# First attention of block 1: heads in pairs, one softplus function, the values' product behind queries and keys, head norms in small steps

## The reference, cut to what matters

```python
h = rms_norm(x, mix_norm_g[l]);  proj = h @ w_in[l]
sb_q, sb_k, sb_v, sw_q, sw_k, sw_v, gate_logits = jnp.split(proj, split_at, axis=-1)
o_sb = stick_breaking_attention(...)      # 8 heads of 64; per head, s < t only:
    z = q k^T * scale
    log_keep = where(strict, -softplus(z), 0)
    tail = reverse cumsum over keys of log_keep, less log_keep
    w = where(strict, exp(log_sigmoid(z) + tail), 0);  o = w v
q = apply_rope(rms_norm(sw_q heads)); k = apply_rope(rms_norm(sw_k heads))
y_swa = sliding_window_sink_attention(q, k, sw_v, sinks[l]) @ w_branch_swa[l]
gates = sigmoid(gate_logits)              # 2 x 1024 columns
x = x + (gates[0] * (o_sb @ w_branch_sb[l]) + gates[1] * y_swa) @ w_out[l]
```

## Time and profile before

| | |
|---|---|
| median of 3 runs | 2334.74 us (2334.29 to 2335.71) |
| profiled execution, its own time | 2335.98 us |
| its span in the profile | 2334.3 us |
| granted TensorE clock, mean | 0.997 of full speed |
| PE / PEld / DVE / ACT / POOL busy | 98 / 86 / 64 / 50 / 8 % |
| mean HBM traffic | 170 GB/s |

### The profile page before, as it was taken

One profiled execution on the slowest core, in us unless ns is written; L12 is line 12 of the kernel. 1 busy time (PEld: TensorE's weight loads), 2 busy tenths in 40 slices (PEclk: granted clock), 3 DMA queues, 4 the chain that ended last, 5 costly groups with the idle time before them and its releaser, 6 DMA issues.

```text
span 2334.3 us, 35415 instructions
## 1 busy us (share of the span) xinstructions
PE 2280.2 (98%) x14356; PEld 2015.2 (86%) x14370; DVE 1489.5 (64%) x2026; ACT 1157.4 (50%) x1785; POOL 198.3 (8%) x191
## 2 busy tenths in 40 slices
PE   7999999999999999999999999999999999999998
PEld 6898888888888888799999878888888999987887
DVE  4557855646874775665667677668655665776774
ACT  4845444574543544545443554445444445355543
POOL 0001200001110210000004001011100000220110
PEclk9999999999999999999999999999999999999999
DMA  7335565533666665554534555566655444364654
GB/s 227 110 115 175 186 201 179 156 112 123 192 189 197 215 191 191 175 177 153 164 100 151 184 165 188 189 208 199 190 175 184 161 158 126 104 215 148 186 185 140
DMA packets 108995, 395.73 MB, mean 170 GB/s; under 512 B 12375, under 2 KB 12545, under 8 KB 108577
## 3 DMA queue, kind: packets, MB, share of 16 engines
q1 hardware_dynamic: 104400, 377.53, 50.7%
q0 software_dynamic: 4432, 15.93, 2.1%
HBM read 392.92 MB, written 1.05 MB: 169 GB/s over the span
## 4 chain that ended last, share of the span: by engine, by line
PE 92%; ACT 4%; DVE 2%; issue 1%; DMA 1%; SPq 0%; DVEq 0%; ACTq 0%
PE psum L409 55%; PE psum L538 17%; PE psum L537 9%; PE psum L837 3%; PE psum L871 2%; PE psum L762 2%; PE psum L855 1%; DMA ring<-in_weights 1%; ACT w_high L363 1%; DVE w_low L366 1%; PE psum L1879 1%; ACT L1338 0%; DVE xT L721 0%; ACT xT L715 0%; DVE x L630 0%
## 5 line engine op out<-in xcount | busy, mean ns | idle before, releaser
L366 DVE TENSOR_TENSOR w_low<-ring,w_high 128x1024 fp32r<-128x1024 f32 x704 | 863.6, 1237 | 512.3 <-ACT w_high L363 510.5
L363 ACT ACTIVATE w_high<-ring 128x1024 fp32r<-128x1024 f32 x704 | 734.5, 1055 | 484.9 <-DMA ring<-in_weights 483.6
L538 PE MATMUL psum<-xT,w_high 128*128 128x512 f32 x1728 | 607.5, 396 | 0.0
L537 PE MATMUL psum<-xT,w_low 128*128 128x256 f32 x1728 | 485.4, 281 | 0.0
L409 PE MATMUL psum<-xT,w_high 128*128 128x256 f32 x2496 | 462.4, 287 | 0.0
L409 PEld LDWEIGHTS psum<-xT,w_high 128*128 128x128 f32 x2496 | 391.6, 193 | 0.8
L538 PEld LDWEIGHTS psum<-xT,w_high 128*128 128x128 f32 x1728 | 324.2, 188 | 77.6
L409 PE MATMUL psum<-w_high,hidden 128*128 128x512 f32 x1216 | 376.7, 390 | 0.0
L409 PE MATMUL psum<-xT,w_low 128*128 128x256 f32 x1248 | 354.4, 284 | 0.0
L537 PEld LDWEIGHTS psum<-xT,w_low 128*128 128x128 f32 x1728 | 326.5, 189 | 0.2
L409 PEld LDWEIGHTS psum<-w_high,hidden 128*128 128x128 f32 x1216 | 228.2, 188 | 47.2
(11 more groups left out here) (237 smaller groups left out, 2309.7 us busy)
## 6 DMA issues: line engine op xcount, KB each, us to landing
ring<-in_weights SPq DMA_DIRECT2D x706, 512.0 KB, 3.6
pages<-in_affine POOLq DMA_DIRECT2D x16, 512.0 KB, 5.8
ring<-in_weights SPq DMA_DIRECT2D x8, 440.0 KB, 3.2
pages<-in_gains POOLq DMA_DIRECT2D x4, 512.0 KB, 4.8
pages<-in_mem POOLq DMA_DIRECT2D x2, 1024.0 KB, 5.6
ring<-in_weights SPq DMA_DIRECT2D x4, 384.0 KB, 3.1
x<-in_x_in SPq DMA_DIRECT2D x2, 512.0 KB, 4.8
pages<-in_rows POOLq DMA_DIRECT2D x2, 512.0 KB, 5.8
```

The costliest lines, as they stand in the source:

```text
L363: eng.activation(high, raw, ACT.Copy).then_inc(self.flag("w_rounded").sem, 1)
L366: eng.tensor_tensor(self.w_low[:, piece % SLOTS, 0:width], raw, high.bitcast(F32), ALU.subtract).then_inc(self.flag("w_split").sem, 1)
L537: pe.matmul(out[:, 0:SEQ], low, self.xT_high[:, k, :], start=(k == 0), stop=False, skip_group_check=True)
L538: m = pe.matmul(out, high, self.xT[:, k, :, :].rearrange("p x s -> p (x s)"), start=False, stop=(k == kn - 1), skip_group_check=True)
```

## The change

The three activations of softplus become one, `ACT.Softplus`, and DVE takes the larger of it and max(z, 0) in place of the sum. Heads go in pairs on all engines: two heads' logits, the values of the two before, a gate, the two heads' sums, a gate. Nine gates stand in the first attention (0 to 8) in place of eleven; gates 10 and 11 go beside the window attention, into steps 1 and 3, and gate 12 into step 5. The product `sbv` goes behind `sbq` and `sbk`, with its pieces in the stream, its banks and its copies on ACT (these now after the roots). `window_heads` yields more often (after the variances, and after the norm of each token tile), and its steps start earlier, from the queries on.

```diff
-GATES_SB = [[0, 1], [2], [3], [4], [5], [6], [7], [8], [9]]
-BESIDE_SWA = {0: [("ysb", 1)], 1: [("gate", 12)], 2: [("ysb", 2)], 4: [("ysb", 3)], 6: [("gate", 13)]}
+BESIDE_SWA = {0: [("ysb", 1)], 1: [("gate", 10)], 2: [("ysb", 2)], 3: [("gate", 11)], 4: [("ysb", 3)],
+              5: [("gate", 12)], 6: [("gate", 13)]}
...
# stream_1, the banks and PE: "sbv" moves from before "sbq" to behind "sbk"; gates in the new order
...
@@ PE
-            for h in range(10):
-                if h < 8:
-                    logits(h)
-                if 1 <= h <= 8:
-                    later_keys(h - 1)
-                if h < 9:
-                    for n in GATES_SB[h]:
-                        gate(n)
-                if h >= 2:
-                    sb_values(h - 2)
-            gate(10)
+            for h in range(0, 8, 2):
+                for x in (h, h + 1):
+                    logits(x)
+                if h:
+                    for x in (h - 2, h - 1):
+                        sb_values(x)
+                gate(h)
+                for x in (h, h + 1):
+                    later_keys(x)
+                gate(h + 1)
+            for x in (6, 7):
+                sb_values(x)
+            gate(8)
...
@@ ACT
             c.root(act, l, c.rsum[:, :, :])
             c.root(act, l, c.fac[:, :, 0:2])
+            split(c.piece_after["sbv"] + AHEAD - 1)
+            for t in range(NT):
+                act.activation(sbv[:, t, :], c.filled(act, l, banks, ("sbv", t)), ACT.Copy ...
...
-                act.activation(b, c.psum[:, 4 + h % 2, 0:SEQ + P], ACT.Abs)...
-                act.activation(b, b, ACT.Exp, scale=-1.0)...
-                act.activation(b, b, ACT.Ln, bias=1.0).then_inc(*c.flag("sb_ln").one())
+                act.activation(soft[:, h % 2, 0:SEQ + P], c.psum[:, 4 + h % 2, 0:SEQ + P], ACT.Softplus
+                               ).then_inc(*c.flag("sb_soft").one())
...
+            for h in range(0, 8, 2):
+                for x in (h, h + 1):
+                    softplus(x)
+                if h:
+                    gate(h - 1)
+                else:
+                    after("sbv")
+                for x in (h, h + 1):
+                    weigh(x)
+                gate(h)
+            gate(7)
+            gate(8)
...
@@ DVE
+            for n in range(2):
+                dve.tensor_scalar(sbqT ... ("sbq", n) ...
+                after(("sbq", n))
+                next(side)
+            for n in range(2):
+                after(("sbk", n))
+                next(side)
             next(side)
...
+            split(c.piece_after["sbv"] + AHEAD - 1)
+            for h in range(0, 8, 2):
+                for x in (h, h + 1):
+                    dve.wait_ge(*c.flag("sb_soft").at(l, x + 1))
+                    if h:
+                        dve.wait_ge(*c.flag("sb_summed").at(l, x - 1))
+                    dve.scalar_tensor_tensor(kept[:, x % 2, ...], psum, 0.0, soft, ALU.max, ALU.max)...
+                after(("gate", h - 1) if h else "sbv")
                 next(side, None)
+                after(("gate", h))
+                next(side, None)
```

More of the change, by code:

```diff
@@ L113, in branch @@
                 s.add(("ysb", n, k), "w_branch_sb", k * P, span(n * P, P), split=True)
-    gates(0, 12)
+    gates(0, 10)
     branch(0, 4)
-    gates(12, 13)
-    branch(4, 8)
-    gates(13, 16)
+    gates(10, 11)
+    branch(4, 6)
+    gates(11, 12)
+    branch(6, 8)
+    gates(12, 16)
     s.matrix("ysw", "w_branch_swa", 512, span(0, D), P, split=True)
@@ L1073, in block_1 @@
     banks, BOTH = Banks(), ("act", "dve")
-    for key in ("swq", "swkv", "sbv"):
+    for key in ("swq", "swkv"):
         for t in range(NT):
             banks.add((key, t))
-    for key, first, end in (("sbq", 0, 2), ("sbk", 0, 2), ("gate", 0, 12), ("ysb", 0, 2), ("gate", 12, 13), ("ysb", 2, 4),
-                            ("gate", 13, 16), ("ysw", 0, 4)):
+    for key, first, end in (("sbq", 0, 2), ("sbk", 0, 2), ("sbv", 0, 2), ("gate", 0, 10), ("ysb", 0, 2), ("gate", 10, 11), ("ysb", 2, 3),
+                            ("gate", 11, 12), ("ysb", 3, 4), ("gate", 12, 16), ("ysw", 0, 4)):
         for n in range(first, end):
@@ L1228, in _ @@
                      swq[:, t, (2 * i + j) * P:(2 * i + j + 1) * P]) for j in range(2) for t in range(NT)])
-            gate(11)
+            gate(9)
             c.wait_read_out(pe, l, "osb0", "osb1")
@@ L1305, in _ @@
             after("swkv")
[L1306 to L1310, removed]
             after(("sbq", 0))
@@ L1321, in _ @@
             c.root(act, l, c.fac[:, :, 0:2])
+            split(c.piece_after["sbv"] + AHEAD - 1)
+            for t in range(NT):
+                act.activation(sbv[:, t, :], c.filled(act, l, banks, ("sbv", t)), ACT.Copy
+                               ).then_inc(*c.drained(banks, ("sbv", t)))
             def softplus(h):
@@ L1426, in after @@
                 split(c.piece_after[key] + AHEAD)
[L1428 to L1439, removed]
             def window_heads():
@@ L1474, in window_heads @@
                         yield
+            c.norm_vector(dve, l, 0, c.x, c.xs,
+                          first_rows if l == 0 else lambda t, n: add("down", l - 1, t, n), gain, None, split, -1,
+                          lambda: dve.wait_ge(*c.flag("gain_in").at(l, 16)))
             side = window_heads()
+            for key in ("swq", "swkv"):
+                after(key)
             next(side)
-            next(side)
[L1480 to L1490, removed]
+            for n in range(2):
+                dve.tensor_scalar(sbqT[:, 2 * n:2 * n + 2, :].rearrange("p k s -> p (k s)"),
+                                  c.filled(dve, l, banks, ("sbq", n)), HD ** -0.5, None, ALU.mult
+                                  ).then_inc(*c.drained(banks, ("sbq", n)))
+                after(("sbq", n))
[3 more added lines that the diff above has]
+                next(side)
+            next(side)
+            split(c.piece_after["sbv"] + AHEAD - 1)
[4 more added lines that the diff above has]
+                        dve.wait_ge(*c.flag("sb_summed").at(l, x - 1))
+                    dve.scalar_tensor_tensor(kept[:, x % 2, 0:SEQ + P], c.psum[:, 4 + x % 2, 0:SEQ + P], 0.0,
+                                             soft[:, x % 2, 0:SEQ + P], ALU.max, ALU.max
+                                             ).then_inc(*c.flag("sb_kept").one())
+                after(("gate", h - 1) if h else "sbv")
                 next(side, None)
+                after(("gate", h))
+                next(side, None)
+            after(("gate", 7))
             for _ in side:
                 pass
-            after(("gate", 9))
             c.settle(dve, l, "dve_step")
@@ L1498, in _ @@
                 dve.tensor_copy(osb[:, t, :], c.psum[:, 6 + t, :]).then_inc(*c.flag("osb_ready").one())
-            after(("gate", 10))
+            after(("gate", 8))
             for i in range(2):
@@ L1504, in _ @@
                             ).then_inc(*c.read_out("dve", "swq0"))
-            after(("gate", 11))
+            after(("gate", 9))
             c.turned(dve, l, "swk")
@@ L2677 @@
          'sb_logits': 8,
-         'sb_ln': 8,
+         'sb_soft': 8,
          'sb_kept': 8,
```

17 lines of the change are left out of this document (7 added, 10 removed).

## The result

The changed kernel took 2314.86 us (median of 4 runs, 2313.13 to 2316.49), the kernel before beside it 2335.22: a ratio of 0.9915, 95% interval 0.9903 to 0.9928, so 19.8 us less. In a later set of runs it took 2312.01 against 2334.73, 0.9907 (0.9894 to 0.9921). Forecast were 2317.3 us, 17.4 less.

What follows compares the result with a forecast made beforehand. PE holds 92% of the chain but waits in the first attention, where ACT sets the pace. Gains 16.4 + 1.8 less 0.8 make 17.4 us, taken from 2334.74: 2317.3 us, range 2314 to 2324.5.

Steps and rivals of the forecast that it cites:

- ACT sets the pace at 5.91 us per head, PE needs 5.5: First attention: ACT has no gap in a head's 5.91 us; PE's own work is 5.48, so it loses 0.43 per head.
- The price of the function: Softplus on ACT: assumed 0.53 us per head, with two table loads per pair, making 7.1 us per pair.
- the bounds: ACT's time per pair: lowest 5.8 us with one load fewer, highest 9.5 with three loads and twice the softplus time.
- The loss in the stage is 16.4 us: Keys' product to output's transposes: PE's work is 52.8 us, so 7.6 and 8.8 are lost in the two layers.
- The window attention gives 1.8: Gate ahead of the last transposes of weights hides their wait, 0.9 by starts per layer; bounds 0 and 2.0 us.
- PE pays 0.8 for changes of kind: Changes between fp32 and rounded products on PE: 0.1 us more per pair, 0.8 for eight pairs.
- The waits inside a pair and ahead of the first maximum hold: First attention: results come 3 and 2.4 us ahead of a pair's sums and next logits; DVE's first maximum has 1.3 cover.
- The first rival: First pair starves on DVE: 1.5 us wait plus 1.7 of lower clock, 3.2 per layer, 2323.7 us; chance 0.14.
- The small steps cost or give nothing: Head norms on DVE: the moved wait for ACT's root costs nothing; alone may gain or lose 0 to about 3 us a layer.
- its likeliest case: The forecast itself, all gains holding and no new wait on PE: 2317.3 us, own range 2315 to 2320; chance 0.70.

Runs made afterwards that it cites:

- softplus_alone: Kernel before with only the one softplus function and the maximum in place of the sum; 2324.28 us, ratio to before 0.9962.
- steps_3_5_empty: Changed kernel with gates 10 and 11 both in step 1 of the window attention, 12 and 13 both in step 6; 2317.61 us, ratio to before 0.9930.
- coarse_norm_steps: Changed kernel with the two new yields taken out and the head norms in the steps of before; 2314.32 us, ratio to before 0.9916.
- pairs_three_functions: Changed kernel with absolute value, exponential and logarithm again in place of softplus, head by head inside each pair; 2335.78 us, ratio to before 1.0007.
- pairs_three_batched: Changed kernel with the three old functions in place of softplus, taken in step for both heads of a pair; 2322.86 us, ratio to before 0.9958.
- vector_late_4b: Changed kernel with four writes of zeros on DVE ahead of the first maxima of each layer; 2322.89 us, ratio to before 0.9958.
- before_again: Kernel before, unchanged, run once more for its trace; the part from the first norm's products to the next layer's norm took 179.77 us.

## Why the prediction was right

*ACT sets the pace at 5.91 us per head, PE needs 5.5.* Right: softplus_alone takes the wait from every head but the first ones. The price of the function was an assumption, since no row showed it; it came out at 0.49 us and two loads per pair, the middle of the bounds.

*The loss in the stage is 16.4 us.* Right. From the first logits on, 59.49 + 60.64, less four gates at 2.96, less 93.46 after, is 14.8; with 1.8 of waits ahead of the first logits, 16.6.

*The window attention gives 1.8.* A little more: 2 x (78.69 + 2 gates at 2.96) less 83.41 and 83.48 is 2.3, of which steps_3_5_empty shows 2.1.

*PE pays 0.8 for changes of kind.* The most mis-sized term: a pair takes 10.99 us, its steps singly 10.96, so next to nothing was to be paid. The sum is then 16.6 + 2.3 = 18.9, as the stages have it (17.1 + 1.8); the forecast was 17.4.

*The waits inside a pair and ahead of the first maximum hold.* Right: no wait of PE in the stage, clock at 1.00, 3.85 us of room on ACT, 1.8 on DVE. The first rival's mechanism exists once the room is used up, but its price was put together otherwise: it took 1.5 us of wait and 1.7 of the lower clock, 3.2 a layer; under load 2.97 us of wait cost 3.3 in the layer whose clock stayed at 1.00 and 6.1 in the one whose clock fell. The Trainium skill ("ScalarE: Activation LUTs", section "What ACT_TABLE_LOAD costs") puts a drain beside each load; no row shows it: here too the load of 103.69 is followed by the tanh at 104.99, 1.30 later.

*The small steps cost or give nothing.* Right (coarse_norm_steps). What I had not seen is which parts matter: function and order alone bring 16.4 of 18.9 us, and the pairs work through the gates that they free.

The first traces of the two kernels are 20.1 us apart. What they have over 18.9 is the 1.2 us by which before was slower from the norm's products to the next norm (181.0 against 179.8), a part that no edit touches. Single executions vary by more than that: the part behind the norm stands at 234.7 or 235.9 us in kernels with the keys first (0.8 more in those with the wait), the part behind both stages of block 1 between 1744.7 and 1749.8. The first trace of before was high in both, the first of after in one. By its number the forecast is right at the edge: 2314.86 lies 0.9 us inside the quick end of its range of 2314 to 2324.5, outside the 2315 to 2320 of its likeliest case, and the later 2312.01 lies below both.

## What to carry to other kernels

When two engines alternate, write down both sums and then walk the chain between them: pairs_three_functions left ACT idle for 1.1 us in each pair and still lost the whole gain. Take out the slower engine's work before rearranging the order; here the order alone gave 2.9 us, the function alone 10.0, both 16.4. Work that only serves as cover should stand where the last wait is: batching heads freed two such pieces, and they were worth 2 us elsewhere; as far as the traces show, the one in step 5 gave all of it.

## What the runs showed of the hardware

The lower clock does not follow from the length of a wait alone. The clock fell behind waits of 1.88 us (softplus_alone, first layer) and 2.34 (pairs_three_batched, both layers), and not behind 2.97 in the first layer of vector_late_4b, whose second layer has a wait of 2.98 (at 445.65) and 0.50 behind it (windows of both layers behind the wait):

```profile
78.00:80.00 2.00, 2.00 (x14) 1.60 (x13) 2.00 (x4) 0.94 (x3) 0.00 (x0) 1.00 0.00 0
82.00:84.00 2.00, 2.00 (x13) 1.53 (x12) 1.19 (x4) 1.05 (x2) 0.00 (x0) 1.00 0.31 43
446.00:450.00 4.00, 4.00 (x12) 2.79 (x12) 3.16 (x6) 1.02 (x3) 0.00 (x0) 0.50 0.02 4
```

So two layers with the same wait differ by 2.9 us: the price of a wait is not fixed by its length, and the clock behind it has to be read.

A part of the kernel that no edit touches (from the first norm's products to the next layer's norm) took 179.8 us in nine traces and 181.0 in five, with nothing between, at a clock of 1.00 and with the same waits (the longest 0.58). Both kernels were seen at 179.8, only the one before at 181.0, but four variants with the new function were there too. The matmuls themselves run in two rhythms. Ten pairs of L537 and L538 lie between these rows of PE's timeline, first in before (181.0), then in before_again (179.8):

```profile
243.63 0.28 PE L537 MATMUL psum<-xT,w_low 128*128 128x256 f32 x1
...
247.17 0.28 PE L537 MATMUL psum<-xT,w_low 128*128 128x256 f32 x1
```

```profile
243.51 0.28 PE L537 MATMUL psum<-xT,w_low 128*128 128x256 f32 x1
...
246.98 0.28 PE L537 MATMUL psum<-xT,w_low 128*128 128x256 f32 x1
```

A pair starts every 0.354 us in the one and every 0.347 in the other. The mean over the 221 such pairs of the stage is 0.353 us in all five traces at 181.0 and 0.348 in all nine at 179.8, which is 1.2 us of difference. The later products of this kind stand at one or the other rhythm too, whatever the kernel, so a part of the spread behind block 1 is of the same origin. What picks the rhythm is open.
